# Moving the sample queries' second group of value products from the causal units into the memory units

## The reference, cut to what matters

```python
def _dilated_sample(q, kc, vc, wb, slopes):   # q (8,4,8,64); kc, vc = window cache of 2048 rows ++ new rows
    for window, dil in DILATED_PATTERNS:      # (128,1), (512,4), (2048,16)
        ...
        s = jnp.einsum('bthd,btnhd->bhtn', q, kg) * ATTN_SCALE
        s = s - slopes[:, None, None] * (i * dil)
        m = jnp.max(s, -1, keepdims=True); p = jnp.exp(s - m); den = jnp.sum(p, -1)
        o = jnp.einsum('bhtn,btnhd->bthd', p, vg) / jnp.swapaxes(den, 1, 2)[..., None]
    return _mix_dilations(outs, lses)         # weights by the softmax denominators

# prompt: the same attention over 1024 rows (group A), causal pooling (B),
# cross-attention into 256 memory tokens with 4 heads (C); then
y = concat(attn, pool, memo) @ w_o
x = LN(alpha * x + y);  x = LN(alpha * x + HMoE(x))   # 4 groups x 8 experts, top-1 then top-2
```

## Time and profile before

| | |
|---|---|
| time, median of 3 runs | 977.32 us (976.07 to 978.16) |
| the profiled execution | 978.47 us, its span 976.7 us |
| TensorE busy in the span | 914.4 us (94%) |
| VectorE, ScalarE, GpSimd busy | 569.8, 390.4, 229.5 us |
| DMA | 273.52 MB, mean 280 GB/s |
| mean granted TensorE clock | 0.97 |

### The profile page before, as it was taken

How to read it: one execution, slowest core, us unless ns; L and a number is a source line. 1 busy time by engine, 2 the same in 40 slices (tenths; PEclk the granted TensorE clock), 3 DMA queues, 4 the chain that set the end, 5 groups by cost and what they waited for, 6 DMA issues and landing times.

```text
span 976.7 us, 13588 instructions
## 1 busy us (share of the span) xinstructions
PE 914.4 (94%) x5214; PEld 651.7 (67%) x5214; DVE 569.8 (58%) x1104; ACT 390.4 (40%) x747; POOL 229.5 (23%) x138
## 2 busy tenths in 40 slices
PE   6999999988998999878999998999999999999984
PEld 6999888964555554546888866666666666666531
DVE  6302021027665656475787677786877777777438
ACT  5202011014655555465110152646455555546236
POOL 0000000079100000021000003265555646464200
PEclk9999999998999999996999997999999999999987
DMA  9999999378977747526756536999999999996286
GB/s 355 310 344 362 348 355 359 128 294 254 331 284 270 265 162 262 174 88 245 256 177 233 195 126 219 315 358 369 358 350 357 348 361 368 370 367 264 77 314 229
DMA packets 54850, 273.52 MB, mean 280 GB/s; under 512 B 13984, under 2 KB 16544, under 8 KB 39680
## 3 DMA queue, kind: packets, MB, share of 16 engines
q1 hardware_dynamic: 46016, 247.97, 70.7%
q0 software_dynamic: 8768, 24.66, 7.1%
HBM read 256.33 MB, written 95.30 MB: 360 GB/s over the span
## 4 chain that ended last, share of the span: by engine, by line
PE 83%; DVE 8%; ACT 4%; issue 3%; DMA 2%; SPq 0%; DVEq 0%; ACTq 0%; POOLq 0%
PE psum L689 76%; PE psum L748 4%; PE psum L979 2%; ACT back L1088 2%; ACT back L521 1%; DVE back L1308 1%; DMA middle<-pair_d 1%; DVE stats L1289 1%; PE psum L892 1%; DVE front L1316 1%; DVE front L1318 1%; PE psum L1002 1%; DVE back L1284 0%; DMA back<-w_in 0%; DMA pair_d<-front,back 0%
## 5 line engine op out<-in xcount | busy, mean ns | idle before, releaser
L1783 POOL DMA_INDIRECT pair_d<-front,back x32 | 134.7, 4209 | 152.7 <-DVE front L1585 152.7
L689 PE MATMUL psum<-back,front 128*64 128x128 f32 (+1 forms) x904 | 152.2, 362 | 5.5 <-ACT back L521 4.6
L689 PEld LDWEIGHTS psum<-back,front 128*64 128x64 f32 (+1 forms) x904 | 71.5, 149 | 61.5 <-issue 51.8
L689 PE MATMUL psum<-gu_high,xg_high 128*112 128x512 f32 x256 | 103.4, 404 | 2.3 <-DVE xg_low L1570 2.3
L689 PE MATMUL psum<-x_high,w_high 128*128 128x352 f32 x288 | 94.2, 327 | 8.3 <-DVE w_low L377 8.3
L689 PE MATMUL psum<-gu_high,xg_low 128*112 128x512 f32 x256 | 100.9, 394 | 0.0
L689 PE MATMUL psum<-gu_low,xg_high 128*112 128x512 f32 x256 | 100.7, 394 | 0.0
L689 PE MATMUL psum<-x_low,w_high 128*128 128x352 f32 x288 | 93.5, 325 | 0.0
L689 PE MATMUL psum<-x_high,w_low 128*128 128x352 f32 x288 | 93.4, 324 | 0.0
L1585 DVE SCALAR_TENSOR_TENSOR front<-psum,back 112x512 f32<-112x512 f32 x64 | 45.1, 747 | 68.8 <-PE psum L689 68.8
L689 PE MATMUL psum<-front 64*128 64x256 f32 (+5 forms) x320 | 77.7, 517 | 3.5 <-DVE stats L1284 2.7
(11 more groups left out here) (220 smaller groups left out, 1723.3 us busy)
## 6 DMA issues: line engine op xcount, KB each, us to landing
back<-w_gu SPq DMA_DIRECT2D x32, 1024.0 KB, 14.2
out_win_k_s<-cache_win_k SPq DMA_DIRECT2D x16, 2044.0 KB, 13.2
out_win_v_s<-cache_win_v SPq DMA_DIRECT2D x16, 2044.0 KB, 12.7
back<-w_down SPq DMA_DIRECT2D x25, 1024.0 KB, 12.9
front<-w_gu SPq DMA_DIRECT2D x16, 1024.0 KB, 11.9
middle<-w_gu SPq DMA_DIRECT2D x16, 1024.0 KB
back<-winkT SPq DMA_DIRECT2D x8, 1792.0 KB, 8.1
back<-cache_win_v SPq DMA_DIRECT2D x8, 1024.0 KB, 7.1
```

The source lines that it names most:

```text
L689: return nc.tensor.matmul(out, lhsT, rhs, start=start, stop=stop, skip_group_check=True)
L1783: G.indirect_dma_start(pair_d, bass.IndirectOffsetOnAxis(ap=IDX[0:CAP, NE + e:NE + e + 1], axis=0), YS[e % 2][0:CAP, :], None, bounds_chec ...
```

## The change

Group 1 of the samples moves later. Before, the steps of units 5 to 31 follow each other without a gap: st of group 1 stands in units 22 and 23, between the parts of pv of group 0, pv of group 1 in 27 to 30, and the last ot in 31. Now pv of group 0 stands in 20 to 23, its ot in 24, st of group 1 in 28 and 30, pv of group 1 in 32 to 35, and its ot in 36; units 25 to 27, 29 and 31 have no step. "ms", "mt", "mpv", "mo" move from 32, 34, 35, 36 to 38, 40, 41, 42, and the four early w_o splits from 40, 42, 44, 46 to 44, 45, 46, 47. PTS of group 1 is no longer beside that of group 0 (in CAT's places of the memory attention) but over a bias table of head pair 2, which VectorE last reads in the minima of unit 23. `o_out` of the first memory unit, which writes over PTS of group 0, waits for pv part 3 of group 0 and no more for that of group 1. No instruction is added or dropped.

```diff
-        PTS = at(18576 + 6 * TOK, 2, 8, P)
+        PTS = [at(18576 + 6 * TOK, 8, P), at(43664, 8, P)]
...
-        WO_SPLIT_AT = {40: 0, 42: 1, 44: 2, 46: 3}
+        WO_SPLIT_AT = {44: 0, 45: 1, 46: 2, 47: 3}
...
         sample_steps = ([("pool", j) for j in range(5)] + [("ss", s) for s in range(6)] + [("st", 0, 0), ("st", 0, 1)]
-                        + [("ss", 6), ("ss", 7), ("pv", 0, 0), ("pv", 0, 1), ("st", 1, 0), ("st", 1, 1)]
-                        + [("pv", 0, 2), ("pv", 0, 3), ("ot", 0)] + [("pv", 1, p) for p in range(4)] + [("ot", 1)])
+                        + [("ss", 6), ("ss", 7)] + [("pv", 0, p) for p in range(4)] + [("ot", 0), None, None, None]
+                        + [("st", 1, 0), None, ("st", 1, 1), None] + [("pv", 1, p) for p in range(4)] + [("ot", 1)])
         for j, e in enumerate(sample_steps):
-            extra[32 - len(sample_steps) + j].append(e)
-        extra[32].append(("ms",))
-        extra[34].append(("mt",))
-        extra[35].append(("mpv",))
-        extra[36].append(("mo",))
+            if e:
+                extra[5 + j].append(e)
+        extra[38].append(("ms",))
+        extra[40].append(("mt",))
+        extra[41].append(("mpv",))
+        extra[42].append(("mo",))
...
-                    act.wait_ge(s_xp, xnum[("pool", 4) if kind == "w" else ("pv", 1, 3)] + 1)
+                    act.wait_ge(s_xp, xnum[("pool", 4) if kind == "w" else ("pv", 0, 3)] + 1)
...
-                        V_.tensor_copy(PTS[:, g, 0:4, :].rearrange("p a b -> p (a b)"), bx).then_inc(s_xe, 1)
+                        V_.tensor_copy(PTS[g][:, 0:4, :].rearrange("p a b -> p (a b)"), bx).then_inc(s_xe, 1)
```

More of the change, by code:

```diff
@@ L816, in x_step @@
                         for b in range(4):
-                            last = mm(bx[32 * b:32 * b + 32, :], PTS[:, g, t, 32 * b:32 * b + 32], vt[:, t % 2, b, :],
+                            last = mm(bx[32 * b:32 * b + 32, :], PTS[g][:, t, 32 * b:32 * b + 32], vt[:, t % 2, b, :],
                                       t == 2 * p, p < 3 and t == 2 * p + 1)
@@ L820, in x_step @@
                         for b in range(4):
-                            last = mm(bx[32 * b:32 * b + 32, :], PTS[0:SMP, g, NVT, 32 * b:32 * b + 32], V[0:SMP, CH - 1, :], False, True)
+                            last = mm(bx[32 * b:32 * b + 32, :], PTS[g][0:SMP, NVT, 32 * b:32 * b + 32], V[0:SMP, CH - 1, :], False, True)
                 elif e[0] in ("ot", "mo"):
@@ L1354, in x_out @@
                     if hf == 0:
-                        V_.tensor_copy(PTS[:, g, 0:4, :].rearrange("p a b -> p (a b)"), bx).then_inc(s_xe, 1)
+                        V_.tensor_copy(PTS[g][:, 0:4, :].rearrange("p a b -> p (a b)"), bx).then_inc(s_xe, 1)
                     else:
-                        step(V_.tensor_copy(PTS[:, g, 4:7, :].rearrange("p a b -> p (a b)"), bx[:, 0:3 * P]))
-                        V_.tensor_copy(PTS[0:SMP, g, 7, :], bx[0:SMP, 3 * P:4 * P]).then_inc(s_xe, 1)
+                        step(V_.tensor_copy(PTS[g][:, 4:7, :].rearrange("p a b -> p (a b)"), bx[:, 0:3 * P]))
+                        V_.tensor_copy(PTS[g][0:SMP, 7, :], bx[0:SMP, 3 * P:4 * P]).then_inc(s_xe, 1)
                 elif e[0] == "pv":
```

## The result

| | before | after |
|---|---|---|
| time, median of 4 runs each | 976.70 us (976.06 to 978.16) | 985.86 us (985.70 to 988.41) |
| the profiled execution | 978.47 us, its span 976.7 | 985.83 us, its span 984.0 |

The ratio, of the means, is 1.0098, with a 95% interval of 1.0077 to 1.0119; between the medians it is slower by 9.2 us, between the two profiled executions by 7.4. The forecast was slower by 3.4, 980.7, with a range up to 984.0. The sign came, the size is out of the range.

A forecast was written before the change was run, and what follows sets the result against it. TensorE seemed the bound in causal units 20 to 31 (68.8 of 71.5 us). Causal units -5.1, memory units +6.4, w_o splits +2.1 gave +3.4 on the median 977.32: 980.7 us, range 975.5 to 984 with rivals.

The forecast's parts named there:

- the transfer: Second memory pair: third pv load lands 7.5 us after issue, so TensorE stalls 1.3 us, bounds 0.8 and 1.9.
- the second hit of the lock: Rival, unit 47: GpSimd's third subtraction gets between the two normalises, T waits 2.35 us more, total 983.1; chance 0.14.
- The pairs: Memory units 32 to 37: three pairs take 8.13, 8.27 and 4.85 us in place of three thin pairs of 16.13.
- the causal units: Units 20 to 31: removed TensorE steps win 5.1 us, with bounds of 4 and 8.65.
- the single hit: Unit 47: the normalise pair waits for one GpSimd subtraction ending at 2.65 us, counted from the transposes of unit 46.
- T46 to T47: Transposes of unit 46 to those of unit 47: 3.15 us, the normalise pair waiting for a GpSimd subtraction.
- T47 to the projection: End of attention: transposes of unit 47 start at 3.15 us, the projection at 9.5, both counted from those of unit 46.
- the ceiling of 8.65: Causal units: 8.15 us of removed pv and ot steps plus 0.5 of waiting in unit 25, if no chain is late.
- the rival in which the change gives back what it takes: Causal units: chains behind TensorE are shorter, 7.5 us won instead of 5.1, total 978.3; chance 0.14.
- the rival of the absorbed steps: Pairs 32 to 37: idle TensorE time absorbs the pv steps, total 973.8 us; decided by a pair under 6.7; chance 0.15.
- the clock stays up: Rival: later steps keep TensorE's clock high up to the projection, 4.0 us could come back, total about 977; chance 0.12.
- the assumption without a row: End of attention: VectorE's subtraction for the concatenation's low part waits for GpSimd, starting at 8.2 us instead of 7.05.

The follow-up runs named there:

- half load: Changed kernel with the third pv load of group 1 bringing one row block (1 MB) instead of two: 980.28 us, ratio 1.0031 against the kernel before.
- The even placement: Changed kernel with group 1's steps moved so that no odd memory unit has one, and two w_o splits (42, 44): 971.74 us, ratio 0.9938 against before.
- the hold: Changed kernel with the last pv load of group 1 issued only when the waited third one has landed: 991.57 us, one run.
- two splits: Changed kernel with two early w_o splits (units 44, 46) instead of four, the others behind the first concatenation cast: 981.85 us, ratio 1.0042 against before.
- the splits alone: Kernel before with only the four w_o splits moved, to units 44 to 47: 980.81 us, ratio 1.0032.
- the third subtraction held: Changed kernel with GpSimd's third subtraction started only after the last normalise of unit 47: 984.67 us, ratio 1.0074 against the kernel before.

## Why the prediction was wrong in size

Three steps failed: the transfer was charged 1.3 and cost 2.6; the fall of the clock behind it was charged nothing and cost 1.5; and the second hit of the lock, priced at 2.35 but left out of the sum as a rival, came. The pairs, the causal units and the single hit were right.

| term | predicted | measured |
|---|---|---|
| causal units, T20 to T32 | -5.1 | -4.9 |
| pair 32-33 | 8.13 | 8.09 |
| pair 34-35 without the transfer | 8.27 | 8.21 (half load) |
| its transfer | 1.3 | 2.6 (2.2 and 2.4 in two other runs), and 1.5 of lower clock |
| pair 36-37 | 4.85 | 4.88 |
| the pairs behind, pushed back | 0 | 0.0 |
| T46 to T47 | +1.1 | +3.4 |
| T47 to the projection | +1.0 | +1.3 |

**Right: the causal units.** Of the ceiling of 8.65 the sum gave back 3.5 to chains behind TensorE, and 3.75 were. Two of them, on TensorE:

```profile
379.88 1.13 PE L690 MATMUL psum<-front 64*128 64x256 f32 x8 [0.93 <-DVE stats L1285]
...
386.88 0.63 PE L749 MATMUL psum<-consts,back 128*128 128x128 f32 x4 [0.51 <-DVE back L1309]
```

The scores of unit 29 wait 0.93 for the minima (1.0 forecast), the transposes of unit 31 wait 0.51 for the normalise (0.5). So the rival in which the change gives back what it takes is out.

**Right: the pairs.** Counted as a ring of exps, copies and waits, they came within 0.1, and the rival of the absorbed steps (a pair under 6.7) fell: 8.09. The even placement shows why it had seemed open: the idle time can be had, but only by a step in an even unit, which doesn't stand behind two exps.

**Wrong: "I take 7.5, so it lands at 11.1: 1.3 of stall".** The step started 8.7 after issue, so the stall of 2.6 is beyond its bound of 1.9. The 7.1 of the earlier trace rows is a median over 1 MB issues, each counted from its own issue. Some of them are a whole load, others one half of a 2 MB load, and only the second half says when such a load is complete. The same load in the kernel before was complete 8.3 after its first issue, so the trace had the number. It was 7.9 to 8.5 in the four traces above that wait for it, with the step 0.2 behind. How much of that the load beside it has (0.2 to 0.6 by the hold) is within what executions differ by.

**Wrong by omission: the clock in the middle.** I had asked whether the clock would stay up before the projection, not whether a new wait could bring it down. It fell 0.9 to 1.2 us after the waiting step had begun, in the changed kernel and in two further runs with that wait (2.80 and 2.40 us), and in the half load, without the wait, it stayed up until 440.7. But with two splits a wait of 2.57 did not bring it down there; it fell 24 us later and cost the same 1.5. So the wait is not enough for a fall at this place. That it causes the fall is argued and not shown; that the fall cost 1.5 is shown. The Trainium skill, "TensorE: Matmul & The Clock Gate", section "HAM oscillation — how this bites in real kernels", describes a wait for a DMA, of 3 to 5 us, after which TensorE runs throttled again; three of the four runs with the wait, of 2.4 to 3.0 us here, agree in the place, the fourth does not. The rival "the clock stays up" is out: 0.50 as the projection starts.

**Wrong: the weight of a rival.** "The lock hits twice" stood at 0.14 with 2.35, and it came true at 2.16. I wrote that the second subtraction ends as the third is ready, and still charged a single hit; such a tie was even odds at best. What broke it was the clock during T and V of unit 46, by 0.8 us. It was low in the half load, in the splits alone and in the held load, with a single hit in each; it was high in the changed kernel, with the double hit, and high with the third subtraction held, where the hit was single again.

**Right: what GpSimd holds.** The single hit (T46 to T47 3.27 to 3.39, forecast 3.15), and the assumption without a row, that the subtraction that makes cat_low waits for GpSimd: 2.29 instead of 1.23, and 1.23 again with two splits, where no subtraction stands beside it. The Trainium skill, "SBUF — State Buffer", section "Who interferes with whom", says that a VectorE instruction with two inputs in SBUF contends with a GpSimd instruction that reads SBUF, and that a tensor_scalar can contend as well; these runs agree on both. My end for it was 0.1 off the measured 1.08 behind GpSimd's.

The miss in sum: 1.3 transfer, 1.5 clock, 2.2 second lock, 0.3 behind unit 47, 0.2 causal, 5.5 of 8.9 - 3.4. The range was too narrow by its own terms: their upper ends (4 won, 7.3 and 4.5 lost) add up to 7.8 slower, or 985.1, and it ended at 984.

**Open:** why the clock falls at one place in one execution and 24 us later in another, and so how often an execution of the changed kernel meets the lock twice: each kernel has one traced execution. Of the four traces with this table of splits and nothing held on GpSimd, one met it twice.

## What to carry to other kernels

What a removed step gives is read from what stands one wait behind it, and what an added one costs, from what it must queue behind: in this kernel the same 1.9 us of matmuls cost 0.4 to 0.6 in an even memory unit and 2.3 to 2.6 in an odd one. A two-slot ring needs a place in the schedule between release and use as long as its slowest landing (here 8.3 to 8.7 us from issue to use for 2 MB with another load behind it), taken from the last issue of a load of the same size and count of issues and not from a median over single issues. Work on a shared port is placed away from the path's VectorE instructions, never twice in a row beside them, and a tie in such a race is charged as if it were lost.

## What the runs showed of the hardware

- A pair of VectorE instructions beside two back-to-back GpSimd subtractions took 3.84 us instead of 0.62: the first took 1.42 and ended with the first subtraction, the second 2.50 and ended with the second. So GpSimd can get in again between two consecutive VectorE instructions. With 0.6 us between the subtractions the pair took 1.68.
- A lower granted clock went with a stretch shorter by 2.0 to 2.2 us in three traces (3.27, 3.27 and 3.39 instead of 5.43 from T of unit 46 to T of unit 47), where the subtraction that would have held the path came later; with the clock high and that subtraction held, the stretch was as short (3.27).
- A load of 2 MB in two issues was complete 7.9 to 8.5 us after the first issue in five traces, while its first half landed after 5.3 to 5.9: the median of single issues says little on the whole.
- A fall of the clock for 3.41 us cost 1.5 us in units 4, 14, 34 or 41, and it isn't a matter of the kernel alone. All four traces from the second chip have a fall in unit 14, and none of the six others has one, with the same instructions up to there. In the last kernel above it fell in units 4 and 14; in the kernel before, in unit 3 instead of 4 and not in 14. The profiled execution of that last kernel, 974.64 us, is 2.9 above its median. A difference of 1.5 us between two profiled executions says nothing until the clock of both has been read.
